# Second mixer of a two-layer backbone: recurrent unit moved under the tiles of the input product, attention with two units' scores in PSUM and the heads' norm in two batches

## The chip, the cores and the metric

The kernel is one program on one core of a Trainium2 chip, written against the engines themselves: each engine (TensorE or PE, VectorE or DVE, ScalarE or ACT, GpSimd or POOL, and SyncE or SP, which issues DMAs) runs its own list of instructions in order, and the lists meet only at semaphores (`wait_ge`, `then_inc`). The metric is the device time of one execution in microseconds (us), as the median of some runs. There are no other cores to wait for.

## What is computed

Two layers over 512 latent and 256 context tokens of width 1024, in fp32. The part that matters here is the mixer of the second layer, between that layer's two half feed-forward blocks:

```python
gate, xr, q, k, v = split(hx @ w_in, (512,) * 5)            # and the same of the context's hc
xr = dwconv_centred(xr, conv_w, conv_b)                     # 4 taps
h  = rglru_bidir(xr, ...)   # r = sigmoid(x wa + ba), i = sigmoid(x wx + bx), a = exp(-8 r softplus(-lam)),
                            # b = sqrt(1 - a^2) * i * x, h_t = a_t h_(t-1) + b_t, both directions, context first
out_c = gelu(gate) * h
q, k = rms_norm(q), rms_norm(k)                             # per head of 64; then rotary embedding
s = q k^T / 8;  p = softmax(s)                              # 4 heads x 2 halves, 512 queries x 768 keys
w = p[:, 0] - lam * p[:, 1];  o = w v
o = rms_norm(o, subln_g) * (1 - lam_init)
y = concat(out_c, o) @ w_out
```

## The kernel before

Activations lie transposed in SBUF: 8 chunks of 128 channels by 768 tokens (`x`, and `xh`, `xl` for the normed input). Every product is done as three fp32r passes: a value is split into a high part (rounded to fp32r) and the rest, and PE adds high x high, low x high and high x low. So each weight tile of 128 columns comes by DMA into `raw`, ACT copies it to `wh` (`split_hi`, line 961, after the product of the tile two places earlier), DVE subtracts to get `wl` (`split_lo`, line 1424), and PE runs the tile (`gemm`): 8 steps k of three passes, into one of two PSUM buffers `G[0]`, `G[1]` (two banks each). Tiles alternate between the two slots, so tile t+2 can start only when ACT and DVE have split its weights and somebody has emptied `G` (`psum_free`). A tile over all 768 tokens is laid out in `HALVES`; one over the 512 latent tokens alone is `LSEG`.

The second mixer is three functions on each engine. `cd_in_*` is the input product, 20 tiles: v, k, q, the recurrent input xr, the gate. Tiles 0 and 1 start on the unnormed input, 2 and 3 are staggered with the norm (`gemm_unnormed`, `gemm_staggered`). Beside the tiles run the turning of v to tokens, the head norms of k and q (`Square` L1281, head sums on PE L815 to L819 into `NP`, `Ln` L1250 and `Exp` L1253 in `rs`, the product in `kq_norm` L1875), the rotary embedding (`swap` L830, `rotate`), the convolution (`conv`, L1898 and L1900) and, at the end, gelu. `cd_mid_*` is everything between the two products. Its order is written out by hand in `SCHED`: for each of four channel groups p of the recurrent unit four attention units with the unit's steps laid between them. A step of the recurrent unit for both directions d: `gates` (PE L849, fp32, sigmoid on ACT L1317), `decay` (exp and tanh, L1325 and L1327), a square on POOL L2159, `comp` (DVE L1948), `root` (sqrt L1332), a product on POOL L2163, `scan` (DVE L1956 to L1968), then `gated`, `hi`, `lo`. The sigmoids of group p+1 wait for the scan of group p (`lru_h`), since they write the same buffers. An attention unit a (a block of 128 queries and a head): both halves' scores on PE (L862, fp32, 64 rows deep, one half in rows 0 to 63 and one in 64 to 127 of the array) into `G[0]` and `G[1]`; DVE's maxima (L1988, one each); two Exp on ACT from PSUM (L1344); on DVE reciprocal, factor and the weighted difference `wb` (L1997, L1999, L2004); six turns on PE (L870); ACT copies them to SBUF (L1350); six products with v (L879); DVE scales the result (L1983); ACT squares and sums it (L1357). Scores of unit a wait for the Exp of unit a-1, because there is one place for them. DVE takes the maxima of a before the difference of a-1. After the last unit all 16 sums of squares go through one Ln and Exp (L1372, L1373), DVE norms four blocks (L2023), PE turns them (L898), DVE and ACT write the second half of the output product's input (L2029, L1376, L2033). `cd_out_*` is the output product, 8 `LSEG` tiles, the first two interleaved; its steps k < 4 need the recurrent half, k >= 4 the attention half.

Each ACT function set must be loaded when it changes (`ACT_TABLE_LOAD`): sigmoid, exp with tanh, sqrt, gelu and Ln have rows of their own.

## Time and profile before

| | us |
|---|---|
| median of 3 runs (2982.64 to 2988.03) | 2984.38 |
| the profiled execution, device time | 2982.56 |
| its span, first to last instruction | 2980.8 |
| PE busy, of the span | 95% |
| DVE, ACT, POOL busy | 52%, 36%, 19% |
| input product of the second mixer, from the end of tile 3 | 2287.0 to 2414.7 |
| between the products | 2414.7 to 2567.4 |
| mean granted TensorE clock | 0.981 |

The profile's page says where the time goes by engine, and which slices of the span have PE below nine tenths; the windows say the same of one stretch. A row of the timeline is: start, duration, engine, line, operation, output and inputs, count, and in brackets the idle time before it and what ended it. A row of the groups is: line, engine, operation, shapes, count, busy time, mean ns of one, idle time before it. Merged rows ("x2", "x6") run from the first start to the last end. An fp32 matmul has two records.

### The profile page before, as it was taken

To read this page: it belongs to the slowest core of one execution; us is meant where nothing else is said; L and a number is where in the kernel's file an instruction comes from. 1 tells how busy PE (TensorE), PEld (TensorE's weight loads), DVE (VectorE), ACT (ScalarE), POOL (GpSimd) and SP (SyncE) were. 2 spreads that over 40 slices of the span, in tenths; PEclk is the share of its full clock that TensorE was granted. 3 is DMA by queue.
4 is the path that set the end of the run, shared out by engine and by line. 5 is a ranking of instruction groups with operands and counts; after the bars stand their busy time and mean duration, and the time that the engine had idled before them with its cause. 6 is when DMAs were issued, how large, how long until landed. Compare 5 with 4: busy or idle time off the path is not lost.

```text
span 2980.8 us, 40958 instructions
## 1 busy us (share of the span) xinstructions
PE 2818.3 (95%) x15780; PEld 2631.5 (88%) x15780; DVE 1549.7 (52%) x2035; ACT 1083.2 (36%) x1514; POOL 570.0 (19%) x294
## 2 busy tenths in 40 slices
PE   5999999999977789999999999999999987799999
PEld 5899999998965778999999999999999855688887
DVE  6964366454556856662565542222246557753333
ACT  3432144236455334441343322112224657442221
POOL 2441044200012721440342100000020113200000
PEclk8999999999999899999999999999999989999999
DMA  7343144111210012441343112111211110123232
GB/s 298 129 159 120 59 152 163 65 50 51 71 42 1 1 36 95 165 166 67 122 153 108 55 64 66 68 56 63 69 58 64 57 57 1 39 92 102 92 97 101
DMA packets 67672, 258.77 MB, mean 87 GB/s; under 512 B 7424, under 2 KB 8576, under 8 KB 66944
## 3 DMA queue, kind: packets, MB, share of 16 engines
q1 hardware_dynamic: 50016, 192.58, 19.4%
q10 hardware_dynamic: 17568, 65.02, 6.3%
q8 instruction: 55, 0.90, 0.1%
q14 instruction: 33, 0.27, 0.0%
HBM read 255.47 MB, written 2.10 MB: 86 GB/s over the span
## 4 chain that ended last, share of the span: by engine, by line
PE 83%; DVE 9%; ACT 2%; issue 2%; POOL 1%; DMA 0%; DVEq 0%; ACTq 0%; POOLq 0%
PE G L450 20%; PE G L452 20%; PE G L454 20%; PE G L457 5%; PE G L459 5%; PE G L461 5%; DVE B L1429 1%; DVE tmp L1613 1%; DVE sL L1829 1%; DVE wl L1424 1%; PE NP L757 1%; PE G L849 1%; DVE xl L1605 1%; PE NP L666 1%; DVE sL L1820 0%
## 5 line engine op out<-in xcount | busy, mean ns | idle before, releaser
L961 ACT ACTIVATE wh<-raw 128x1024 fp32r<-128x1024 f32 (+1 forms) x300 | 338.9, 1130 | 1540.5 <-PE G L454 1227.4
L450 PE MATMUL G<-xh,wh 128*128 128x384 f32 x2624 | 673.8, 337 | 34.3 <-DVE wl L1424 21.9
L452 PE MATMUL G<-xl,wh 128*128 128x384 f32 x2624 | 670.2, 336 | 0.0
L454 PE MATMUL G<-xh,wl 128*128 128x384 f32 x2624 | 669.2, 336 | 0.0
L1424 DVE TENSOR_TENSOR wl<-raw,wh 128x1024 fp32r<-128x1024 f32 (+1 forms) x300 | 427.0, 1423 | 379.5 <-ACT wh L961 378.7
L450 PEld LDWEIGHTS G<-xh,wh 128*128 128x128 f32 x2624 | 474.8, 189 | 40.8 <-DVE wl L1424 19.0
L452 PEld LDWEIGHTS G<-xl,wh 128*128 128x128 f32 x2624 | 477.3, 189 | 0.0
L454 PEld LDWEIGHTS G<-xh,wl 128*128 128x128 f32 x2624 | 476.9, 189 | 0.0
L2094 POOL TENSOR_TENSOR mraw<-mraw,scb 128x1024 f32<-128x1024 f32 x120 | 315.0, 2625 | 646.7 <-DVE B L1429 646.7
L454 PE MATMUL G<-hh,wl 128*128 128x384 f32 x1056 | 268.1, 334 | 0.0
L452 PE MATMUL G<-hl,wh 128*128 128x384 f32 x1056 | 268.1, 334 | 0.0
L450 PE MATMUL G<-hh,wh 128*128 128x384 f32 x1056 | 268.0, 334 | 0.0
L1429 DVE SCALAR_TENSOR_TENSOR B<-mraw,scb 128x1024 f32<-128x1024 f32 x120 | 235.2, 1960 | 0.0
L1531 DVE SCALAR_TENSOR_TENSOR x<-G,modG,x 128x256 f32<-128x256 f32 x112 | 49.0, 479 | 349.3 <-PE G L454 349.3
L1459 DVE TENSOR_TENSOR tmp<-tmp,G 128x768 f32<-128x768 f32 x64 | 61.1, 954 | 284.8 <-PE G L454 284.8
L457 PE MATMUL G<-xh,wh 128*128 128x512 f32 (+1 forms) x528 | 199.7, 388 | 2.8 <-DVE wl L1424 2.8
L461 PE MATMUL G<-xh,wl 128*128 128x512 f32 (+1 forms) x528 | 197.6, 384 | 0.0
L459 PE MATMUL G<-xl,wh 128*128 128x512 f32 (+1 forms) x528 | 197.6, 384 | 0.0
L452 PEld LDWEIGHTS G<-hl,wh 128*128 128x128 f32 x1056 | 190.7, 188 | 0.0
L450 PEld LDWEIGHTS G<-hh,wh 128*128 128x128 f32 x1056 | 190.7, 188 | 0.0
L454 PEld LDWEIGHTS G<-hh,wl 128*128 128x128 f32 x1056 | 190.6, 188 | 0.0
L977 ACT ACTIVATE mraw<-mraw 128x1024 f32<-128x1024 f32 x120 | 126.3, 1053 | 42.3 <-ACT mraw L977 23.6
(332 smaller groups left out, 3256.8 us busy)
## 6 DMA issues: line engine op xcount, KB each, us to landing
raw<-in_w SPq DMA_DIRECT2D x176, 512.0 KB, 3.5
mraw<-in_wmn ACTq DMA_DIRECT2D x120, 512.0 KB, 4.5
raw<-in_w SPq DMA_DIRECT2D x64, 704.0 KB, 4.0
raw<-in_abin SPq DMA_DIRECT2D x24, 512.0 KB, 3.5
raw<-in_cdin SPq DMA_DIRECT2D x20, 512.0 KB, 3.5
mini<-in_wmn SPq DMA_DIRECT2D x9, 512.0 KB, 14.8
gmini<-in_wmn SPq DMA_DIRECT2D x2, 2048.0 KB, 21.9
raw<-in_about SPq DMA_DIRECT2D x8, 512.0 KB, 3.5
```

Of the source, the lines that this page charges most:

```text
L450: pe.matmul(bank(h), W, tokens(rh, h), start=(k == 0), stop=False)
L452: pe.matmul(bank(h), W, tokens(rl, h), start=False, stop=False)
L454: mm = pe.matmul(bank(h), L, tokens(rh, h), start=False, stop=(k == nk - 1))
L457: pe.matmul(G[slot][:, a:b], W, rh[:, k, a:b], start=(k == 0), stop=False)
L459: pe.matmul(G[slot][:, a:b], W, rl[:, k, a:b], start=False, stop=False)
L461: mm = pe.matmul(G[slot][:, a:b], L, rh[:, k, a:b], start=False, stop=(k == nk - 1))
L961: act.activation(wh[slot][:, 0:nk * P], raw[slot][:, 0:nk * P], ACT.Copy).then_inc(hi_done, 1)
L977: act.activation(mraw[:, j, :], mraw[:, j, :], ACT.Copy, accum_out=M[:, bass.ds(it * 3 + (24 + j), 1), 1:2].rearrange("p a s -> p (a s)")) ...
L1424: dve.tensor_tensor(wl[slot][:, 0:nk * P], raw[slot][:, 0:nk * P], wh[slot][:, 0:nk * P].bitcast(F32), ALU.subtract).then_inc(lo_done, 1)
L1429: return dve.scalar_tensor_tensor(B67[:], tile, 1.0, scv[:, s, :], ALU.mult, ALU.mult, accum_out=out)
L1459: dve.tensor_tensor(by_block(hf[:, 0:T]), by_block(g1s[:, 0:T]), from_banks(G[1], 0, T), ALU.mult).then_inc(psum_free[1], 1)
L2094: pool.tensor_tensor(mraw[:, j, :], mraw[:, j, :], scb[:, 1, :], ALU.mult).then_inc(mod_prod, 1)
```

## The change

All of it is in the second mixer.

- The tiles of the input product come in the order xr, gate, k, q, v (0 to 3, 4 to 7, 8 to 11, 12 to 15, 16 to 19). Convolution and recurrent unit run beside tiles 2 to 13: each engine's steps stand in a list by tile c; PE's gate matmuls, head sums, swaps and two of four turns of v stand between steps k of a tile, at places given by four tables. The gate matmuls go into `NP` and `B67`. `SCHED` is gone.
- DVE now waits in `cd_in` for the scan of a group before it empties the next tile's PSUM, since the list is in order. POOL does its eight rotary products after all its products of the recurrent unit.
- The weights of the gates come as six DMAs into the unused ends of `raw`, `wh`, `wl`, ahead of tile 4's weights.
- The constants' arithmetic and its two small Exp move into the feed-forward block before.
- In the attention the eight banks are cut anew: three banks of scores for even units, three for odd ones (`SC`), and `B67` for turns and values. Scores are six matmuls of 256 keys, alternating between the two halves and never in the same bank, in two parts around `values(a - 3)`. One maximum instruction takes both halves. DVE's order is: difference of a-1, scaling of a-3, maxima of a. A turn waits for the scaling of the unit before (`on_done`), a copy on ACT goes ahead of the Exp.
- The norm of the heads is done for units 0 to 11 at once while the last units run and for the last four after them; the last block is turned between steps 3 and 4 of the output product. ACT and DVE write the output product's input straight from PSUM. The recurrent half of it lies in `gateh` and `hsuml`.

```diff
+        lruw = [at(f"lruw{q}", [P, FH * P - D], MR + 3 * D + q * FH * P + D) for q in range(6)]
...
+        banks = ctx.enter_context(nc.psum_tensor("banks", [P, 4096], F32))
+        G = [banks[:, 1024 * s:1024 * s + 1024] for s in range(2)]
+        NP, B67 = banks[:, 2048:3072], banks[:, 3072:4096]
+        SC = [banks[:, 1536 * q:1536 * q + 1536] for q in range(2)]
...
-        SCHED = []
...
+        GATES_IN = {4: 0, 7: 1, 9: 2, 11: 3}
+        SUM_AT = {(10, 3): 0, (12, 2): 1, (13, 4): 2, (14, 4): 3, (15, 2): 4, (16, 2): 5, (17, 2): 6, (18, 2): 7}
+        SWAP_AT = {(13, 5): 0, (14, 5): 1, (15, 6): 2, (16, 4): 3, (17, 1): 4, (18, 0): 5, (19, 0): 6, (19, 6): 7}
+        TURN_AT = {(19, 2): 0, (19, 5): 1}
...
+            load_tiles(CD + 2, 2, dr["cdin"], KC, 2)
+            for q in range(6):
+                wq = FH * P - D
+                n = min(wq, 16 * P - q * wq)
+                sp.dma_start(lruw[q][:, 0:n], dr["lruw"][:, q * wq:q * wq + n]).then_inc(lruw_landed, 16)
+            load_tiles(CD + 4, CD_IN_T - 4, dr["cdin"], KC, 4)
...
+            def gates(p_, d):
+                e = 2 * p_ + d
+                if e == 0:
+                    pe.wait_ge(lruw_landed, 96)
+                pe.wait_ge(cv_ready, 8 + p_ + 1)
+                if e == 6:
+                    pe.wait_ge(kq_ln, 8 + 1)
+                for g in range(2):
+                    if e:
+                        pe.wait_ge(gate_sig, 2 * (e - 1) + g + 1)
+                    m = 8 * g + 4 * d + p_
+                    for a, b, _s in SEGS:
+                        mm = pe.matmul((NP, B67)[g][:, a:b], lruw[m // 3][:, m % 3 * P:m % 3 * P + P], xc[:, p_, a:b],
+                                       start=True, stop=True)
+                    mm.then_inc(gate_mm, 1)
...
+            def head_sum(i):
...
+                if i < 4:
+                    pe.wait_ge(sql_set, 8 + i + 1)
+                    for a, e, _s in SEGS:
+                        pe.matmul(NP[:, a:e], blkr[:], sqh[:, a:e], start=True, stop=False)
+                        mm = pe.matmul(NP[:, a:e], blkr[:], sql[:, a:e], start=False, stop=True)
...
+                for c in range(4, CD_IN_T):
+                    def under(k):
+                        if c in GATES_IN and k in (2, 6):
+                            gates(GATES_IN[c], k // 4)
+                        if (c, k) in SUM_AT:
+                            head_sum(SUM_AT[c, k])
+                        if (c, k) in SWAP_AT:
+                            swap(SWAP_AT[c, k])
+                        if (c, k) in TURN_AT:
+                            turn_v(TURN_AT[c, k])
+                    gemm(CD + c, c % 2, (CD + c) // 2, KC, xh, xl, LSEG if 4 <= c < 8 or 12 <= c < 16 else HALVES, under)
...
+                def scores(a, part):
...
+                        if (s, b_) == (1, 0):
+                            pe.wait_ge(s2_bank, a + 1)
+                        mm = pe.matmul(SC[a % 2][:, T * s + b_:T * s + b_ + 256], q2[hp, h, P * qt:P * qt + P],
+                                       k2[hp, h, b_:b_ + 256], start=True, stop=True)
+                        if (s, b_) == (0, 512):
+                            mm.then_inc(s2_bank, 1)
+                    if part:
                         mm.then_inc(s2_done, 1)
...
                 def turn(a):
                     pe.wait_ge(w_done, a + 1)
                     if a:
-                        pe.wait_ge(wt_ready, a)
+                        pe.wait_ge(on_done, a)
+                    else:
+                        pe.wait_ge(v2_ready, 4)
...
+                for a in range(NA2 + 3):
+                    if a < NA2:
+                        scores(a, 0)
+                    if 3 <= a:
+                        values(a - 3)
+                    if a < NA2:
+                        scores(a, 1)
+                    if a == 0:
+                        turn_v(2)
+                        turn_v(3)
+                    if 2 <= a <= NA2 + 1:
+                        turn(a - 2)
+                    if a == NA2 + 1:
+                        turn_o(0)
+            def turn_o(qt):
+                pe.wait_ge(onr_done, qt + 1)
+                if qt >= 2:
+                    pe.wait_ge(cd_cat2, qt - 1)
+                for h in range(4):
+                    mm = pe.transpose(NP[:, 512 * (qt % 2) + P * h:512 * (qt % 2) + P * h + P], onq[qt][:, P * h:P * h + P],
+                                      cst("ident"))
+                mm.then_inc(oq_done, 1)
...
+                    if f == 2 and h == 0:
+                        act.wait_ge(dl_set, 1)
+                        act.activation(coef[:, 1, :], coef[:, 0, :], ACT.Exp, scale=-1.0).then_inc(coef_exp, 1)
+                        act.wait_ge(dl_set, 3)
+                        act.activation(dl[:, 2:4], dl[:, 0:2], ACT.Exp).then_inc(dl_exp, 1)
...
+                act.wait_ge(xn_ready, 40)
+                act.wait_ge(coef_set, 1)
+                for c in range(2, CD_IN_T):
+                    split_hi(CD + c + 2, c % 2, (CD + c + 2) // 2, KC)
+                    if c < 4:
+                        evac(c)
+                    if 4 <= c < 8:
+                        gelu(c - 4)
+                    if c == 2:
+                        add_bias(0)
+                    if c == 3:
+                        gates(0)
+                    if c == 4:
+                        root(0)
+                        add_bias(1)
+                        add_bias(2)
+                    if c == 5:
+                        add_bias(3)
+                    if c == 6:
+                        gates(1)
+                        hi(0)
+                    if c == 7:
+                        root(1)
+                    if c == 8:
+                        squares(0)
+                        squares_hi(0)
+                        gates(2)
+                        hi(1)
+                    if c == 9:
+                        root(2)
+                        squares(1)
+                        rs(0)
+                        squares_hi(1)
+                    if c == 10:
+                        gates(3)
+                        squares(2)
+                        hi(2)
+                    if c == 11:
+                        root(3)
+                        rs(1)
+                        squares_hi(2)
+                    if c == 12:
+                        rs(2)
+                        squares(3)
+                        squares_hi(3)
+                        hi(3)
+                    if 13 <= c < 18:
+                        rs(c - 10)
+                    if 13 <= c < 17:
+                        squares(c - 9)
+                    if c == 18:
+                        copy_v(0)
+                        copy_v(1)
...
                 def att(a):
...
                     if 2 <= a <= NA2 + 1:
                         act.wait_ge(tr2_done, a - 1)
                         if a >= 4:
                             act.wait_ge(pv2_done, a - 3)
-                        act.activation(wtb[a % 2][:], NP[:, 0:T], ACT.Copy).then_inc(wt_ready, 1)
+                        act.activation(wtb[a % 2][:], B67[:, 0:T], ACT.Copy).then_inc(wt_ready, 1)
+                    if a < NA2:
+                        act.wait_ge(max2_ready, a + 1)
+                        if a >= 2:
+                            act.wait_ge(w_done, a - 1)
+                        for s in range(2):
+                            act.activation(pr2[a % 2][s][:], SC[a % 2][:, T * s:T * s + T], ACT.Exp, bias=st2[:, a % 4, s:s + 1],
+                                           accum_out=st2[:, a % 4, 2 + s:3 + s]).then_inc(p2_ready, 1)
                     if a >= 4:
...
+                        head_squares(a - 4)
...
+                copy_v(2)
+                for a in range(NA2):
+                    att(a)
+                    if a == 0:
+                        copy_v(3)
+                head_norm(0, 12)
+                att(NA2)
+                att(NA2 + 1)
+                hi(0)
+                head_squares(NA2 - 2)
+                hi(1)
+                head_squares(NA2 - 1)
+                head_norm(12, 16)
+                hi(2)
+                hi(3)
...
+                dve.wait_ge(xn_ready, 40)
+                for q in range(2):
+                    for a, b in ((0, 2), (514, 517), (773, 774)):
+                        dve.memset(xpad[q][:, a:b], 0.0)
+                for q in range(2, 4):
+                    ins = dve.memset(xpad[q][:], 0.0)
+                ins.then_inc(pad_zero, 1)
+                conv(0)
+                for c in range(2, CD_IN_T):
+                    if c >= 8:
+                        evac(c)
+                    split_lo(CD + c + 2, c % 2, KC)
+                    if c in (2, 3):
+                        conv(c - 1)
+                    if c == 4:
+                        comp(0)
+                        conv(3)
+                    if c == 5:
+                        scan(0)
+                    if c == 6:
+                        gated(0)
+                    if c == 7:
+                        comp(1)
+                        lo(0)
+                        scan(1)
+                    if c == 8:
+                        squares_lo(0)
+                        gated(1)
+                    if c == 9:
+                        comp(2)
+                        lo(1)
+                        scan(2)
+                    if c == 10:
+                        squares_lo(1)
+                        kq_norm(0)
+                        gated(2)
+                    if c == 11:
+                        comp(3)
+                        lo(2)
+                        scan(3)
+                    if c == 12:
+                        squares_lo(2)
+                        kq_norm(1)
+                        gated(3)
+                    if c == 13:
+                        squares_lo(3)
+                        lo(3)
+                    if 13 <= c < 19:
+                        kq_norm(c - 11)
+                        rotate(c - 13)
+                    if c >= 18:
+                        rotate(c - 12)
...
+                for a in range(NA2 + 2):
+                    if 1 <= a <= NA2:
+                        weigh(a - 1)
+                    if a >= 3:
+                        out(a - 3)
+                    if a < NA2:
+                        biggest(a)
+                    if a == NA2:
+                        normed(0)
+                normed(1)
+                normed(2)
+                out(NA2 - 1)
+                out_lo(0)
+                out_lo(1)
+                normed(3)
+                out_lo(2)
+                out_lo(3)
...
-    order = [(4 * gw, 5 * gw), (3 * gw, 4 * gw), (2 * gw, 3 * gw), (gw, 2 * gw), (0, gw)]
+    order = [(gw, 2 * gw), (0, gw), (3 * gw, 4 * gw), (2 * gw, 3 * gw), (4 * gw, 5 * gw)]
```

## Rows read from the trace of the kernel before

**Rows 1.** Windows: busy us (instructions) of each engine, granted clock, DMA share, GB/s.

```profile
2287.00:2414.60 127.60, 126.32 (x641) 111.81 (x639) 70.29 (x91) 71.22 (x86) 11.97 (x8) 1.00 0.24 78
2414.60:2568.00 153.40, 110.99 (x499) 71.78 (x499) 106.57 (x142) 109.28 (x181) 43.29 (x24) 0.87 0.01 4
```

**Rows 2.** Timeline, PE, at the two edges of the stretch between the products.

```profile
2416.41 2.82 PE L849 MATMUL G<-xc,lruw 128*128 128x512 f32 x8 [1.74 <-issue]
...
2579.38 0.39 PE L461 MATMUL G<-xh,wl 128*128 128x512 f32 x1
```

**Rows 3.** Timeline of attention units between the products: DVE, ACT and PE.

```profile
2504.13 1.80 DVE L1988 TENSOR_REDUCE st<-G 128x1 f32<-128x768 f32 x2
...
2505.10 0.90 ACT L1344 ACTIVATE pb<-G,st 128x768 f32<-128x768 f32 x1 [1.01 <-DVE st L1988]
...
2506.29 1.02 DVE L2004 SCALAR_TENSOR_TENSOR wb<-pb,st,pb 128x768 f32<-128x768 f32 x1
2506.78 0.20 ACT L1344 ACTIVATION_READ_ACCUMULATOR pb<-G,st 128x1 f32 x1
...
2506.87 0.81 ACT L1350 ACTIVATE wtb<-NP 128x768 f32<-128x768 f32 x1
...
2507.83 0.34 DVE L1983 TENSOR_SCALAR onq<-B,st 128x128 f32<-128x128 f32 x1
...
2530.46 1.57 PE L862 MATMUL G<-k,q 64*128 64x512 f32 x8
...
2531.96 0.87 PE L870 MATMUL NP<-con,wb 128*128 128x128 f32 x6
...
2532.67 1.50 PE L879 MATMUL B<-vtok,wtb 128*128 128x128 f32 x12
```

**Rows 4.** Timeline, DVE, at the end of the attention: the wait for the heads' norm.

```profile
2562.46 2.50 DVE L2023 TENSOR_TENSOR onq<-onq,hrs 128x512 f32<-128x512 f32 x4 [3.69 <-ACT hrs L1373]
```

**Rows 5.** Timeline of the recurrent unit's steps between the products.

```profile
2419.31 0.90 ACT L1317 ACTIVATE lR<-G,par 128x768 f32<-128x768 f32 x1
2420.26 2.85 PE L849 MATMUL G<-xc,lruw 128*128 128x512 f32 x8 [1.04 <-ACT lR L1317]
...
2430.32 0.93 ACT L1327 ACTIVATE lR<-lR,coef 128x768 f32<-128x768 f32 x1
...
2502.13 1.81 DVE L1948 SCALAR_TENSOR_TENSOR lR<-lX,lR 128x768 f32<-128x768 f32 x2
...
2507.98 1.28 ACT L1332 ACT_TABLE_LOAD   x1
2509.27 1.58 ACT L1332 ACTIVATE lR<-lR 128x768 f32<-128x768 f32 x2
2510.20 4.28 POOL L2163 TENSOR_TENSOR lI<-lI,lR 128x768 f32<-128x768 f32 x2 [8.80 <-ACT lR L1332]
2510.26 2.55 DVE L2004 SCALAR_TENSOR_TENSOR wb<-pb,st,pb 128x768 f32<-128x768 f32 x1
...
2519.05 1.28 ACT L1317 ACT_TABLE_LOAD   x1 [4.03 <-DVE hsum L1968]
```

**Rows 6.** Timeline beside the input product: splits, convolution and head norm.

```profile
2397.15 3.14 DVE L1900 SCALAR_TENSOR_TENSOR cb<-pad,par,cb 128x771 f32<-128x771 f32 x3
...
2398.42 1.06 ACT L961 ACTIVATE wh<-raw 128x1024 fp32r<-128x1024 f32 x1 [2.66 <-PE G L461]
...
2400.21 1.22 DVE L1424 TENSOR_TENSOR wl<-raw,wh 128x1024 fp32r<-128x1024 f32 x1
...
2403.86 1.06 ACT L961 ACTIVATE wh<-raw 128x1024 fp32r<-128x1024 f32 x1 [0.50 <-PE G L461]
```

**Rows 7.** Timeline, PE, after a wait for split weights.

```profile
2272.76 0.80 PE L450 MATMUL G<-xh,wh 128*128 128x384 f32 x2 [1.60 <-DVE wl L1424]
...
2276.51 0.51 PE L450 MATMUL G<-xh,wh 128*128 128x384 f32 x2
2276.86 0.51 PE L452 MATMUL G<-xl,wh 128*128 128x384 f32 x2
```

More of the change, by code:

```diff
@@ L206, in build @@
         wtb = [at(f"wtb{q}", [P, T], ATT[q] + 3 * T) for q in range(2)]
-        ovb = [at(f"ovb{s}", [P, 512], TB + s * T) for s in range(2)]
         fw = [FREE]
@@ new lines, in turn_o, with step @@
+            def turn_o(qt):
[6 more added lines that the diff above has]
+                mm.then_inc(oq_done, 1)
+            def cd_out_pe():
+                def step(s, k):
+                    return gemm_step(s, k, KC, gateh if k < 4 else xh, hsuml if k < 4 else xl, LSEG)
+                for s in range(2):
+                    weights_ready(CDO + s, s, CDO // 2)
+                turn_o(1)
+                turn_o(2)
+                for k in range(KC):
@@ L1360, in cd_mid_act @@
-                for what, i in SCHED:
-                    if what == "gates":
-                        gates(i)
-                    if what == "decay":
-                        decay(i)
-                    if what == "root":
-                        root(i)
-                    if what == "hi":
-                        hi(i)
-                    if what == "att":
-                        att(i)
-                act.wait_ge(ss_ready, NA2)
-                chain(act.activation(hsq[:, 1, :], hsq[:, 0, :], ACT.Ln, bias=eps[:, 0:1], scale=1.0 / P))
```

478 lines of the change are left out of this document (195 added, 283 removed).

## Prediction

> **What bounds it now.** I read the windows first, then the timeline at their edges, then single units of work. Beside the input product PE is the bound: from the end of tile 3 it is busy 126 of 127.6 us, ACT 71, DVE 70 [rows 1]. Between the products nothing is full: in 153 us PE is busy 111 at a mean clock of 0.87, ACT 109, DVE 107 [rows 1]; there the lists wait for one another. The stretch begins at 2414.7 (1.74 us before its first matmul) and with the first two output tiles, which both kernels interleave, ends at 2579.8 [rows 2]: 165.1 us. So work taken out of it and laid beside the tiles pays twice where PE has room, and costs PE time one for one where it hasn't.
>
> **Part 1, the attention alone.** I follow one unit through the new order. DVE takes the maxima of unit a in one instruction; two of 768 last 1.80 us, one of 1536 I take as 1.70 (bounds 1.6 and 1.8). From the first Exp's start to the end of the second's sum ACT needs 1.88 us; from the end of maxima over reciprocal and factor to the end of the difference DVE needs 1.38; the scaling 0.34, of which 0.26 stands ahead of the next instruction [rows 3]. In DVE's new list the difference of a stands before the maxima of a+1, and waits for both Exp of a. So a second place for scores frees PE, but not the chain maxima, Exp, Exp, difference, scaling, maxima: 1.70 + 1.88 + 1.38 + 0.26 and two hand-overs between DVE and ACT of 0.06 each are 5.35 us a unit (5.1 to 5.7). Everything else fits in: PE needs 1.6 + 0.75 + 1.5 = 3.9 [rows 3]; turn (0.9) and copy (0.7) run while DVE takes the maxima, and end about when these do, so they add 0 to 0.3. The Trainium skill (TensorEngine Tiling (Array Packing), Restrictions and Gotchas) says that different row tiles cannot access the same PSUM bank at the same time; the new six-part order keeps to that, and eight score records in 1.57 us show the halves side by side; had they to go one after the other, 2.6 us, PE would still fit.
>
> First maxima: PE is free of tile 19, DVE empties it (1.1), splits a tile (1.2) and does the last rotation (1.4): 3.8 us after tile 19. Then 15 periods, two of them without scaling: 3.8 + 2 x 5.1 + 13 x 5.35 = 83.6. From the last unit's maxima on: Exp 3.6; the square of the unit before and the first batch's norm, 3.7 as now [rows 4], to 7.4; copy 8.0, values and scaling of 14 to 10.1, turn, copy, values and scaling of 15 to 13.9; two turns of blocks and eight steps of the output product (0.68 each) to 20.7, under which the second batch's norm (to 18.4) hides; the last block's turn, copy and difference hold PE 1.6; the rest ends at 28. So 112 us against 165.1: **-53.3** (-48 to -56).
>
> **Part 2, what PE gets beside the tiles.** Eight times two gate products at 2.8 us [rows 5]: +22.4. Two of four turns of v go the other way (-1.6). Head sums, swaps, tiles are the same number. **+20.8.** The constants go beside the feed-forward block, where DVE and ACT have idle time; the two Exp bring two table loads: nothing on the path (1 us at most, if a weight split came behind them). The six DMAs stand on SP's queue ahead of tile 4's weights, which are wanted some 10 us later: nothing.
>
> **Part 3, who waits beside the tiles.** ACT's list from tile 4 to step 4 of tile 13 holds 9 splits (1.0), 16 sigmoids (0.8 to 0.9), 16 exp and tanh (0.93), 8 square roots (0.8), about 18 loads (1.28) [rows 5, 6] and some 16 us of gelu, bias, squares and norms: 82 us. PE's own work there is 87 us, tiles, gates and two head sums. So nearly each us that ACT waits for somebody is one that PE waits. I walk the lists with those durations, in us from the start of tile 4. A tile is 5.44 (`LSEG`, the time from one split's start to the next's, [rows 6]) or 24 pairs of passes at 0.35 [rows 7], split high 1.06 and low 1.22, conv 3.8 [rows 6]. POOL and DVE hold each other: the difference L2004, 1.02 alone, takes 2.55 beside POOL's product [rows 5, 3], it ends 0.8 after the first of two 1.8 us products; a scan queued at the same time waits for the second.
> - Group 0: gates end at 9, ACT's chain of exp and tanh at 15. Only then come the high part of tile 6 and gelu, at 18. PE has finished tile 5 at 16: **2.0**. Square root, then two biases; the last conv waits for the first of these, the low part of tile 7 for the conv: 28.3, PE waits **4.8**.
> - Group 1: scan of group 0 ends 33, sigmoids behind it, exp and tanh done 45, root 51, POOL 55, scan 59. Tile 8 is finished at 49, and DVE's copy of it stands behind the scan, ACT's square behind the copy, the sigmoids of group 2 behind the square: the gates at step 6 of tile 9 wait 57.8 to 64.2: **6.4**.
> - Groups 2 and 3: the gates of group 3 wait for a Ln that reads `NP`: **1.0**. Scan of group 2 ends 87; of group 3, 112. Tile 12 is finished at 101; PE waits **1.4** for tile 13's low part, then at step 4 for the head sum 2, whose operand DVE makes behind that scan, a copy and a split, at 115: **10.2**. Head sum 3 waits **1.5** in tile 14. From tile 15 on ACT keeps up.
> These are 27.3. Behind a wait of 1.60 us PE runs at its lower level, 1.2 GHz: a pair of passes takes 0.80, and 0.51 again (2.4 GHz) only 3.75 us later [rows 7], which has cost about 1.7 us. Behind the other wait shown, 1.74 us [rows 2], it ran at the upper one. I charge 1.7 to each of the three waits over 4 us: 5.1. Sum **+32.4**; bounds: 16, if every second wait is covered by something that I put too late, and 46.
>
> A rule of the Trainium skill speaks against this part: ScalarE: Activation LUTs, What ACT_TABLE_LOAD costs, gives 1283 ns and a drain of about 1380 ns more for each switch. Here the instruction behind a load starts 1.29 us after it [rows 5]: the trace has the first part and not the second. Were the drain paid in the walk's list, its 13 loads more than now would add 18 us.
>
> **Sum.** 2982.56 (the profiled execution, 1.8 under the median of the runs) - 53.3 + 20.8 + 32.4 = 2982.5. I take **2982**: what the attention gives, the input product takes.
>
> **Rivals.**
> - *The recurrent round is shorter than I walk it* (0.32). For it: PE is the bound of the input product now, its lists have slack, and 27 us of waits rest on four places where one list stands behind another, each of which goes if gelu, conv, the copy of tile 8 or the operand of head sum 2 comes 4 to 10 us earlier. Against: sigmoids of p+1 can't start before the scan of p, 16.8 us after the gates even without other work (0.9 + 1.28 + 3.7 + 2.1 + 0.8 + 3.6 + 4.5) [rows 5]. Waits of 16: 2966; none at all: 2950.
> - *VectorE and GpSimd hold each other on the path* (0.28, slower). POOL has 24 instructions of 1.5 to 1.8 us in the walk, DVE's splits, comp and head norm read two operands from SBUF. Today most meet beside waits. If eight more of DVE's path instructions queue behind one of POOL's at 1.5 us, +12, and one more restart at the lower clock, +1.7: 2996. It decides from about four such meetings (+6).
> - *The change doesn't do what it says in the attention*: the two places for scores don't shorten the chain. That is in my sum. Were they to (4.6 a unit, PE and DVE alone), -12: 2970. I give it 0.05, within the first.
>
> **How the numbers follow.** Walk as computed 0.40, within 6 us mostly (faster 0.10, same 0.24, slower 0.06); first rival 0.32 (0.28, 0.04, 0); second 0.28 (0, 0.06, 0.22). Faster 0.38, same 0.34, slower 0.28, where 0.2% (6 us) is what a measurement of this kernel tells from no change. Signs are mixed: the likeliest case alone has 2974 to 2990. The range for 8 in 10 reaches to the other cases: 2957 to 3004.
>
> **What would show it.** Between the products: Exp to Exp 5.35 us apart, PE not the one waited for, clock near 1; 112 us from tile 19 to the end of the second output tile. Beside the input product: 181 us instead of 127.7 from tile 4 on; PE waits for `wl` before tile 7, for a sigmoid in tile 9, for `sql` in tile 13, the last the longest; ACT busy nearly throughout up to tile 13. I am wrong if PE has no wait over 3 us there (then 2960 or less), or if the units come more than 6 us apart (then over 2993).

## The result and the profile after

The changed kernel takes 2990.22 us (median of 20 runs, 2985.55 to 2993.08), the kernel before 2984.56 in the same comparison (20 runs, 2981.75 to 2988.03): ratio 1.0017, 95% interval 1.0010 to 1.0023. It is 5.7 us slower. I had said 2982 and called a gain a little likelier than a loss, so the sign was wrong and the size off by 8; the range of 2957 to 3004 holds it. A second comparison gave 2989.68 against 2983.61, 1.0021 (1.0012 to 1.0030). The profiled execution of the changed kernel is one of its short ones, 2985.62 us (span 2983.8); to that of before (2982.56) it is +3.06, where my sum had -0.1. Two single executions of variants below, 8424.85 us (head sum 2's operand) and 4028.16 us (passes for nothing), lie in a slower state and bear on nothing; without them the medians of these two fall by 0.1 and 0.2.

Windows of the changed kernel (from, to, span; busy us and instructions of TensorE; granted clock; DMA share; GB/s): from the start of tile 4 to the end of the input product, then to the end of the second output tile. They answer to [rows 1] and [rows 2].

```profile
2287.00:2467.00 180.00, 152.53 (x691) 0.94 0.16 50
2467.00:2583.00 116.00, 89.55 (x559) 0.96 0.02 5
```

180 us instead of 127.7, and 116 instead of 165.1: more exactly they are 180.8 (2286.57 to 2467.37) and 115.5 (to 2582.86), and I had walked 181 and 112. What TensorE waited for between 2284 and 2620 (line that waits <- what it waits for: us in total, times, longest; `onq` is a unit's scaled result, `sql` the low part of the squares for a head sum, `wl` the low part of a tile's weights, `lR` a sigmoid's output):

```profile
PE banks L889 <- DVE onq L2161: 15.7, 14, 3.2
PE banks L811 <- DVE sql L2035: 12.0, 2, 10.7
PE banks L453 <- DVE wl L1516: 8.5, 4, 4.8
PE banks L798 <- ACT lR L1340: 6.1, 1, 6.1
```

The waits beside the input product one by one (timeline, TensorE: start, us, operation, [idle before <- releaser]):

```profile
2305.11 0.47 PE L453 MATMUL banks<-xh,wh 128*128 128x512 f32 x1 [2.15 <-ACT gate L1317]
2315.65 0.79 PE L453 MATMUL banks<-xh,wh 128*128 128x512 f32 x1 [4.84 <-DVE wl L1516]
...
2351.19 5.23 PE L798 MATMUL banks<-xc,lruw 128*128 128x512 f32 x8 [6.06 <-ACT lR L1340]
2370.77 2.82 PE L798 MATMUL banks<-xc,lruw 128*128 128x512 f32 x8 [1.13 <-issue]
2390.13 0.50 PE L453 MATMUL banks<-xh,wh 128*128 128x512 f32 x1 [1.21 <-DVE wl L1516]
2403.93 0.77 PE L811 MATMUL banks<-sqh,blkr 128*128 128x512 f32 x1 [10.74 <-DVE sql L2035]
2413.99 0.47 PE L811 MATMUL banks<-sqh,blkr 128*128 128x512 f32 x1 [1.26 <-DVE sql L2035]
```

In this order they are tile 6, tile 7, gates in tile 9, gates of group 3, tile 13, head sum 2 and head sum 3: walked 2.0, 4.8, 6.4, 1.0, 1.4, 10.2, 1.5. The second number of a row is how long the pass behind the wait takes. For one pass of 512 columns 0.79 and 0.77 are the lower clock level, 0.39 to 0.50 the upper; for the eight records of the gates 5.23 and 2.82.

A unit of the attention (timeline, VectorE, ScalarE and TensorE; it answers to [rows 3]):

```profile
2504.75 1.75 DVE L2167 TENSOR_REDUCE st<-banks 128x2 f32<-128x1536 f32 x1
2504.98 0.85 PE L889 MATMUL banks<-con,wb 128*128 128x128 f32 x6 [0.88 <-DVE onq L2161]
2505.86 0.81 ACT L1424 ACTIVATE wtb<-banks 128x768 f32<-128x768 f32 x1 [2.51 <-PE banks L889]
2506.57 0.90 ACT L1430 ACTIVATE pb<-banks,st 128x768 f32<-128x768 f32 x1
2507.45 0.90 ACT L1430 ACTIVATE pb<-banks,st 128x768 f32<-128x768 f32 x1
2508.47 0.17 DVE L2148 RECIPROCAL st<-st 128x2 f32<-128x2 f32 x1 [1.98 <-ACT pb L1430]
2508.93 1.02 DVE L2155 SCALAR_TENSOR_TENSOR wb<-pb,st,pb 128x768 f32<-128x768 f32 x1
2509.86 0.35 DVE L2161 TENSOR_SCALAR onq<-banks,st 128x128 f32<-128x128 f32 x1
2510.12 1.75 DVE L2167 TENSOR_REDUCE st<-banks 128x2 f32<-128x1536 f32 x1
```

Maxima, Exp, Exp, reciprocal, difference, scaling, maxima: 2504.75 to 2510.12, 5.37 us (walked 5.35), and the copy behind the turn ends about when the Exp starts (2506.67 and 2506.57).

### The profile page after: what moved, and what is told of

Same layout as the page of the kernel before. It is cut to its first block, busy times and chain, and to the rows that moved or that the text cites. A ratio compares the mean times of both kernels' runs of the same rounds, so it can differ in the third digit from the quotient of the medians.

```text
span 2983.8 us, 41082 instructions
## 1 busy us (share of the span) xinstructions
PE 2810.1 (94%) x15844; PEld 2631.5 (88%) x15844; DVE 1540.4 (52%) x2023; ACT 1111.1 (37%) x1531; POOL 571.5 (19%) x294
## 4 chain that ended last, share of the span: by engine, by line
PE 81%; DVE 9%; issue 3%; ACT 3%; POOL 1%; DMA 0%; DVEq 0%; ACTq 0%; POOLq 0%
PE banks L446 20%; PE banks L450 20%; PE banks L448 20%; PE banks L453 5%; PE banks L457 5%; PE banks L455 5%; DVE banks L1521 1%; DVE wl L1516 1%; DVE tmp L1705 1%; DVE sL L1925 1%; DVE xl L1697 1%; PE banks L798 1%; ACT pb L1430 1%; PE banks L753 1%; PE banks L662 1%
## 5 line engine op out<-in xcount | busy, mean ns | idle before, releaser
L446 PE MATMUL banks<-xh,wh 128*128 128x384 f32 x2624 | 675.9, 338 | 32.0 <-DVE wl L1516 20.1
L448 PE MATMUL banks<-xl,wh 128*128 128x384 f32 x2624 | 669.8, 336 | 0.0
L450 PE MATMUL banks<-xh,wl 128*128 128x384 f32 x2624 | 669.3, 336 | 0.0
L446 PEld LDWEIGHTS banks<-xh,wh 128*128 128x128 f32 x2624 | 474.8, 189 | 41.5 <-DVE wl L1516 17.7
L448 PEld LDWEIGHTS banks<-xl,wh 128*128 128x128 f32 x2624 | 477.2, 189 | 0.0
L450 PEld LDWEIGHTS banks<-xh,wl 128*128 128x128 f32 x2624 | 477.1, 189 | 0.0
L448 PE MATMUL banks<-hl,wh 128*128 128x384 f32 x1056 | 267.9, 334 | 0.0
L446 PE MATMUL banks<-hh,wh 128*128 128x384 f32 x1056 | 267.9, 334 | 0.0
L450 PE MATMUL banks<-hh,wl 128*128 128x384 f32 x1056 | 267.8, 334 | 0.0
L1521 DVE SCALAR_TENSOR_TENSOR banks<-mraw,scb 128x1024 f32<-128x1024 f32 x120 | 237.4, 1978 | 0.0
```

The costliest lines, as they stand in the source:

```text
L446: pe.matmul(bank(h), W, tokens(rh, h), start=(k == 0), stop=False)
L448: pe.matmul(bank(h), W, tokens(rl, h), start=False, stop=False)
L450: mm = pe.matmul(bank(h), L, tokens(rh, h), start=False, stop=(k == nk - 1))
L1521: return dve.scalar_tensor_tensor(B67[:], tile, 1.0, scv[:, s, :], ALU.mult, ALU.mult, accum_out=out)
```

## The experiments

Four reorderings of the changed kernel, run together. Since executions differ by 1 to 3 us before tile 4 already, I compare two stretches of the profiles as well: from the start of tile 4 to the first scores (2286.57 to 2468.46 in the changed kernel, 181.9), and from there to the step k = 4 of the output product (to 2577.12, 108.7). By the medians the first three reorderings are 5.0, 6.7 and 5.9 us under the changed kernel's 2990.22, where the expectations had 6 to 9, 3 to 5 and about 4; that median is of another comparison (the kernel before had 2984.56 there and 2983.83 here), and the medians hold the changing clock of other places too, so I go by the first stretch.

**Head sum 2's operand ahead of the scan.**

```diff
 ScalarE, c == 11:  -root(3) rs(1) squares_hi(2)   +rs(1) squares_hi(2) root(3)
 ScalarE:           -hi(3) at c == 12              +hi(3) at c == 13
 VectorE, c == 11:  -comp(3) lo(2) scan(3)         +comp(3) lo(2) squares_lo(2) kq_norm(1)
 VectorE, c == 12:  -squares_lo(2) kq_norm(1) gated(3)   +scan(3) squares_lo(3) gated(3)
```

> The operand of head sum 2 is made in front of the scan of group 3 (ScalarE: Ln, Exp and high part of the squares in front of the last square roots; VectorE: the low part in front of scan(3), the gated product of group 3 and its high part later). My walk: in the changed kernel TensorE stands 10.7 us in tile 13 for sql; here sqh is ready near 2393.9 and sql near 2394.9 on the clock of that profile, TensorE's wait becomes about 1.8, head sum 3 waits about 2 instead of 1.3, and the kernel is about 8 us faster than the changed one (6 to 9), at about 2982. If the wait is not from the order of the lists but from VectorE and GpSimd holding each other, scan(3) and the product before it only move and sql is late again: the wait stays over 6 us and the time within 3 us of the changed kernel.

2985.21 us (before 2983.83), the first stretch 178.6: 3.3 less, where I had expected 8 (6 to 9).

```profile
2395.63 0.47 PE L811 MATMUL banks<-sqh,blkr 128*128 128x512 f32 x1 [1.91 <-DVE sql L2036]
2408.75 0.77 PE L811 MATMUL banks<-sqh,blkr 128*128 128x512 f32 x1 [5.82 <-DVE sql L2036]
```

The wait for head sum 2 went from 10.7 to 1.9 as walked, so this wait came of the order. But head sum 3 now waits 5.8 (I had said 2): its operand stands behind the moved scan, and GpSimd's products run beside three of that scan's four passes, which take 2.33, 2.14 and 1.69 instead of 0.68, 1.28 and 0.67. Half of the 8.8 us was a debt to the next sum.

**Tile 8's copy in front of scan(1).**

```diff
+                    if c == 8:
+                        scan(1)
                     split_lo(CD + c + 2, c % 2, KC)
...
                     if c == 7:
...
-                        scan(1)
```

> VectorE copies tile 8 out of PSUM in front of scan(1) instead of behind it. My walk: ScalarE's squares and their high part no longer stand between the end of the scan (2346.2) and the sigmoids of group 2, which start there instead of at 2350.1; TensorE's wait in tile 9 falls from 6.1 to about 2.2 us, everything behind it keeps its distances, so about 4 us faster than the changed kernel (3 to 5), 2986. If the walk is wrong and the wait rests on the gates' own chain (exp, tanh, root, product, scan) alone, the wait stays at 5 to 6 and the time moves by under 1.5 us.

2983.48 us; first stretch 178.6, 3.3 less; TensorE's wait in tile 9 is 3.54 instead of 6.06 (I had expected 2.2), and the gate products behind it run at the upper clock (2.82 instead of 5.23):

```profile
2352.34 2.82 PE L798 MATMUL banks<-xc,lruw 128*128 128x512 f32 x8 [3.54 <-ACT lR L1340]
```

**The last convolution behind the low part of tile 8.**

```diff
 VectorE:  -conv(3) behind comp(0), c == 4      +conv(3) in front of gated(0), c == 6
 ScalarE:  -add_bias(3) at c == 5               +add_bias(3) behind gates(1), c == 6
```

> The last convolution goes behind the low part of tile 8 and the scan of group 0 in VectorE's list, its bias on ScalarE behind the gates of group 1. My walk: the low part of tile 7 is ready at 2312.1 instead of 2315.6, TensorE's wait there 4.8 -> 1.3 us, scan(0) and with it all later groups come 3.6 us earlier: 3.6 us, and 1 more if the restart at the lower clock (0.63 instead of 0.39 a pass) goes with it: 2985 to 2987. If the chain of the groups were not what sets the later waits, the gain would be eaten in tile 9, whose wait would grow from 6.1 to over 9 us: no change in the time.

2984.36 us; first stretch 178.5, 3.4 less. Tile 7 waits 2.09 now (expected 1.3), for gelu, and tile 9 waits the same 6.08 as before the edit: the gain was not taken back, so the chain of the groups sets the later waits and moved with the scan.

```profile
2315.15 0.47 PE L453 MATMUL banks<-xh,wh 128*128 128x512 f32 x1 [2.09 <-ACT gate L1317]
2350.34 4.89 PE L798 MATMUL banks<-xc,lruw 128*128 128x512 f32 x8 [6.08 <-ACT lR L1340]
```

**Maxima in front of the weights.**

```diff
+                    if a >= 3:
+                        out(a - 3)
+                    if a < NA2:
+                        biggest(a)
                     if 1 <= a <= NA2:
                         weigh(a - 1)
-                    if a >= 3:
-                        out(a - 3)
-                    if a < NA2:
-                        biggest(a)
```

> In the attention VectorE takes the maxima of unit a in front of the weights of unit a-1 (scaling of a-3, maxima of a, reciprocal, factor and difference of a-1). My theory: the unit's period of 5.37 us is the chain maxima, Exp, Exp, difference, scaling, maxima; with the new order the maxima of a run beside the Exp of a-1, no chain closes within one unit, and TensorE is the bound (scores 1.6, turn 0.75 to 0.9, values 1.6): period 4.0 to 4.3 us, 15 times 1.2 = 18 us less, at 2971 to 2974. Rival: not the chain but something shared (PSUM banks, the copy between turn and values, values behind scaling) sets it: period over 4.9, 7 us or less.

2970.06 us against 2983.83 before (0.9955, 0.9942 to 0.9967), 20 less than the changed kernel. Through the middle units TensorE works without a gap, and a unit takes 4.46 us (2500.32 to 2504.78), a little over the 4.0 to 4.3 I expected because the scores take 2 x 1.06 and not 1.6:

```profile
2500.32 1.13 PE L875 MATMUL banks<-k,q 64*128 64x256 f32 x6
2501.38 0.88 PE L889 MATMUL banks<-con,wb 128*128 128x128 f32 x6
2502.18 1.13 PE L875 MATMUL banks<-k,q 64*128 64x256 f32 x6
2503.24 1.60 PE L896 MATMUL banks<-vtok,wtb 128*128 128x128 f32 x12
2504.78 1.13 PE L875 MATMUL banks<-k,q 64*128 64x256 f32 x6
```

So the 5.37 us was the chain, closed by VectorE's order alone. The second stretch is 90.3, 18.4 less, and that this is my 15 x 1.2 is partly luck: from the first maxima to the last, twelve periods give 0.91 each, the first three units 5.2, and 2.1 is a fall of the clock in the changed kernel (below) that doesn't come here.

**The changed kernel once more.**

> The changed kernel, unaltered, beside the others of this call. Its twenty times lay in two groups, seven from 2985.6 to 2987.2 and thirteen from 2988.4 to 2993.1, and its profile is of the lower one (2985.6). If the groups belong to the kernel, its median is again 2989 to 2991 and a profile of the upper group shows 3 to 5 us more at one place: by my theory of the clock at TensorE's restarts (passes at 0.63 instead of 0.39 us behind a wait) that is one or two waits more that are followed by the lower clock, between 2284 and 2600. If they belong to the chip or the hour, the median is near 2986.

2989.68 us (ten runs, 2987.4 to 2992.3), and this profile is of a long execution, 2990.95: 5.3 us over the other. No single place has them: tile 4 starts 1.4 later, the first stretch is 1.2 longer, the second 1.1, the rest 1.6. The last is seen best. Both profiles wait 1.9 us for the weights of the second pair of output tiles; in the first one all passes behind take 0.39 to 0.50, in this one:

```profile
2588.47 0.50 PE L453 MATMUL banks<-gateh,wh 128*128 128x512 f32 x1 [1.90 <-DVE wl L1516]
...
2589.35 0.63 PE L453 MATMUL banks<-gateh,wh 128*128 128x512 f32 x1
...
2592.68 0.40 PE L457 MATMUL banks<-gateh,wl 128*128 128x512 f32 x1
```

3.3 us at the lower level, which costs 1.6. The same wait is followed by the lower level in one execution and not in the other. The twenty executions of the changed kernel say the same as a whole: the mean granted clock is 0.982 to 0.985 in the seven that take under 2988 us, and 0.978 to 0.983 in the thirteen above. So the two groups belong to the kernel, as I expected.

**Passes for nothing in two waits.**

```diff
+            def fill(n):
+                for _ in range(n):
+                    pe.matmul(NP[:, 0:512], blkr[:], xh[:, 0, 0:512], start=True, stop=True)
...
+                if i == 2:
+                    fill(37)
...
+                    if c == 7:
+                        pe.wait_ge(gate_sig, 4)
+                        fill(19)
```

> The changed kernel with passes whose result nobody reads laid into two of TensorE's waits: 19 in front of tile 7 (wait 4.8 us) and 37 in front of head sum 2 (10.7 us), at 0.23 us each, so that they end before what TensorE waits for is there. The waits' ends stay where they are. By the theory of the restart the passes behind them then last 0.39 us from the first on instead of 0.63 to 0.79, which is worth 1.2 to 1.7 us at each place: 2.5 to 3.5 us less in the profile, and if the upper group of the times is made by restarts, the spread goes and the median is 2984 to 2986. If the clock is not what makes the difference, the time stays within 1 us of the changed kernel's median of the same call.

2986.45 us, 3.2 less than the changed kernel beside it. The passes behind both waits run at the upper level from the first on (0.79 and 0.77 before):

```profile
2311.17 4.60 PE L804 MATMUL banks<-xh,blkr 128*128 128x512 f32 x19
2316.17 0.50 PE L453 MATMUL banks<-xh,wh 128*128 128x512 f32 x1 [0.40 <-DVE wl L1525]
...
2394.18 8.90 PE L804 MATMUL banks<-xh,blkr 128*128 128x512 f32 x37 [1.80 <-ACT ssq L1303]
2403.11 0.50 PE L817 MATMUL banks<-sqh,blkr 128*128 128x512 f32 x1
...
2412.53 0.47 PE L817 MATMUL banks<-sqh,blkr 128*128 128x512 f32 x1 [2.09 <-DVE sql L2044]
...
2413.45 0.63 PE L453 MATMUL banks<-xh,wh 128*128 128x512 f32 x1
```

By the end of tile 14's passes in front of head sum 3 TensorE is 3.0 us ahead of the changed kernel, as expected of the clock (2.5 to 3.5). But there it waits 2.09 instead of 1.26, and behind this wait the clock falls, which it did not in the changed kernel's profile, and takes 1.6 back. So the first stretch is 181.4, only 0.5 less than in the short profile of the changed kernel and 1.7 less than in the long one. The passes for nothing keep the clock up where they stand, and the next wait can take the gain again; that the medians are 3.2 apart is more than these profiles show. The spread stayed (2983.4 to 2989.3), since the other waits are left, and the median lies above the 2984 to 2986 that I had expected.

**The product in front of the scans on VectorE.**

```diff
 GpSimd:   -lI[d] = lI[d] * lR[d]   for d in 0, 1
 VectorE:  +lI[d] = lI[d] * lR[d]   for d in 0, 1, at the head of scan(p_)
```

> The product in front of the scans (beta times gated input, two of 768 columns per group) goes from GpSimd (1.8 us each) to VectorE. It tests the rival of VectorE and GpSimd holding each other: in the changed kernel the first scan lasts 2.3 us instead of 0.68 in groups 1, 2 and 3, queued behind GpSimd's second product. On VectorE the two products take 1.0 each, the second right behind the first, and the four scans follow: the end of the group's scans comes 1.5 to 2 us earlier in groups 0 to 3. Since the groups' chain sets the waits of tile 9 and head sum 2, TensorE's waits shrink by the same and the sum is 4 to 7 us less than the changed kernel. If the chain did not set them, nothing changes (within 1 us).

2979.72 us (0.9988 of before, 0.9979 to 0.9997), 10 less than the changed kernel beside it (expected 4 to 7); first stretch 175.5, 6.4 less. Of the changed kernel, then of this one (GpSimd and VectorE, group 1):

```profile
2338.11 3.61 POOL L2323 TENSOR_TENSOR lI<-lI,lR 128x768 f32<-128x768 f32 x2 [5.04 <-ACT lR L1352]
2339.97 2.30 DVE L2064 TENSOR_TENSOR_SCAN lX<-lA,lI 128x256 f32<-128x256 f32 x1 [2.40 <-POOL lI L2323]
```

```profile
2337.26 1.83 DVE L2062 TENSOR_TENSOR lI<-lI,lR 128x768 f32<-128x768 f32 x2 [0.51 <-ACT lR L1352]
2339.00 0.68 DVE L2068 TENSOR_TENSOR_SCAN lX<-lA,lI 128x256 f32<-128x256 f32 x1
```

The scan of 256 columns takes 0.68, and 2.30 while GpSimd's second product runs: it ends at 2342.27, 0.55 us behind GpSimd's products (2341.72). TensorE's waits in tile 7, tile 9 and at head sum 2 fell by 1.7, 1.7 and 2.5.

**The unit left out.**

```diff
-        GATES_IN = {4: 0, 7: 1, 9: 2, 11: 3}
+        GATES_IN = {}
...
-    conv, add_bias, gates, root (ScalarE), comp, scan, GpSimd's products
+    gated: hsum = gate * gate
```

> The changed kernel without the recurrent unit: the gate products, sigmoids, exp, tanh, roots, convolutions, scans and GpSimd's three products per group are left out (the square of the gelu stands in for the unit's output, its split and the six weight transfers stay). Tiles, head sums, swaps and the whole attention are as in the changed kernel. It prices the second side of my sum by itself. By the walk the unit costs 22.4 us of TensorE and 32.4 of waits and restarts beside the tiles: 54.8 less, 2935, with 127 from the start of tile 4 to the first scores instead of 181.9, and no wait of TensorE over 1.6 us there. By the changed kernel's trace (gate pair 2.39 apart, waits 28.0) 19.1 + 28.0 + 2 to 5: 49 to 52 less, 2938 to 2941. If the input product had waits of its own under the unit's (splits, head norms with their table loads), 40 or less: over 2950.

2932.08 us, 58 less by the medians and 53.7 by the profiles; tile 4 to first scores is 129.5, 52.4 less. I had walked 54.8, the trace had given 49 to 52. Two waits for `sql` are left, 2.8 together, the longer 2.1, where I had said none over 1.6 (us in total, times, longest):

```profile
PE banks L809 <- DVE sql L2031: 2.8, 2, 2.1
```

**All together.** The diffs are those above: first the four reorderings, then these and the product on VectorE.

> The four reorderings together (operand of head sum 2 in front of scan(3); copy of tile 8 in front of scan(1); last convolution behind tile 8's low part; maxima in front of the weights). Each alone took, between the start of tile 4 and the first scores, 3.1, 3.3 and 3.4 us, and the last one 18.4 between the first scores and the output product. If they rest on different waits they add: 28 us less than the changed kernel, about 2961. If they share waits (what the convolution gives is taken again in tile 9 or at head sum 2), 22 to 24 us: 2966.

2960.38 us. The stretches are 172.2 and 90.3: 9.7 and 18.4 less, where each alone gave 3.3, 3.3, 3.4 and 18.4. They rest on different waits.

> The four reorderings of the run with all of them, and the product in front of the scans on VectorE. If the shortened chain of a group still sets the waits that are left (2.1 in tile 7, 3.5 in tile 9, 4.2 at head sum 3), it gives most of what it gave alone, 6.4 us between the start of tile 4 and the first scores: 2954. If the reorderings have used the same slack, 2 to 3: 2958.

2956.18 us, **0.9908 of before (0.9894 to 0.9922)**, first stretch 167.5: 4.7 less than the last one, between the two expectations.

The other tail, on top of that:

```diff
 ScalarE:  -head_norm(0, 12) att(16) att(17) hi(0) head_squares(14) hi(1) head_squares(15) head_norm(12, 16) hi(2) hi(3)
           +att(16) att(17) head_squares(14) head_squares(15) head_norm(0, 16) hi(0) hi(1) hi(2) hi(3)
 TensorE:  -turn_o(0) turn_o(1) turn_o(2), k = 0 to 3, turn_o(3), k = 4 to 7
           +k = 0 to 3, turn_o(0) turn_o(1) turn_o(2) turn_o(3), k = 4 to 7
 VectorE:  -normed(0) before the last two out(), out_lo(0) out_lo(1) before normed(3)
           +out(15), normed(0) to normed(3), out_lo(0) to out_lo(3)
```

> As the run before it, with another end of the attention: one head norm for all sixteen heads instead of two batches, behind the copy of the last unit, and the four first steps of the output product in front of the turns of the heads' output. In the changed kernel ScalarE's Ln, Exp and their two table loads stand between the last Exp and the copy of unit 14, and TensorE waits 3.2 us there, with its passes at the lower clock behind it (values of unit 14 2.5 to 2.9 us instead of 1.6). By my theory of the tail the copy of 14 comes 3.5 us earlier, the last values end near 4.5 us earlier, the four steps (5.5 us) cover the norm, and the step for k = 4 starts 3.5 to 4.5 us earlier: 4 us less. Rival: the norm of the last unit and the chain of four turns, copies and differences is longer than the four steps, and what was saved ahead is waited for behind: 1 us or less, or slower.

2956.27 us, no gain (expected 4 less). The second part did get shorter, 87.8 against 90.3, but behind the new waits for the turned blocks (1.2 and 1.6) stands

```profile
2544.55 0.50 PE L453 MATMUL banks<-xh,wh 128*128 128x512 f32 x1 [1.56 <-DVE xl L2178]
...
2545.62 0.63 PE L453 MATMUL banks<-xh,wh 128*128 128x512 f32 x1
```

and seven passes in all take 0.63, which gives 1.5 of the 2.5 back. The first stretch is 1.4 longer than in the run before, by another such fall: the gates of tile 9 take 4.51 behind a wait of 2.02, and in the run before 2.82 behind the same wait. So the rival had the number, 1 us or less, but its mechanism only in part: the new waits cost some of what I had hoped for, and the clock, in this profile, the rest.

## Why the prediction was right, and where it was wrong

- *What bounds the kernel, and part 3's walk*: right. The seven waits beside the tiles sum to 27.4 (walked 27.3), each in its place and behind the work I had named; tile 4 got one more of 0.56. Three reorderings moved three of them, the run without the unit all but 2.8. The charge of 5.1 for restarts held as well: against the same passes at the upper level, those behind the waits lose 1.3 in tile 7, 2.4 in tile 9 and 1.5 at head sum 2, 5.2 together. From tile 4 to the end of the product it is 180.8, walked 180.9; that this fits to 0.1 is partly luck, see part 2.
- *Part 2*: the eight records of two gate products last 2.8, but they overlap with what stands behind: the second tile pass starts 2.81 after the first of them (2323.79 to 2326.60), where the tile's own step is 0.23. So a pair costs 2.6 and eight of them 21, and 22.4 was 1.6 too high. Some 1.8 us that I had in no term, such as first passes behind waits of 0.47 to 0.50 instead of 0.39, made it up; I have not placed all of them.
- *Part 1, the unit*: right. 5.37 for 5.35, with the chain as named, and the counter-test of the maxima's place (4.46).
- *Part 1, the rest*: **this is the step that failed.** I wrote that TensorE needs 3.9 of the 5.35 us and "everything else fits in", and charged restarts at the lower clock to three waits beside the tiles and to none in the attention. TensorE's own need is 4.46, which at the upper clock still fits: in ten units it waits 0.88 and the period stays 5.37. But behind the wait of 3.23 between the fourth maxima and the fifth its clock fell to the lower level (granted clock 0.83 between 2480 and 2500, 1.00 between 2500 and 2520), and that unit took 7.5:

```profile
2486.53 1.75 DVE L2167 TENSOR_REDUCE st<-banks 128x2 f32<-128x1536 f32 x1
2486.76 1.51 PE L889 MATMUL banks<-con,wb 128*128 128x128 f32 x6 [3.23 <-DVE onq L2161]
2488.20 2.07 PE L875 MATMUL banks<-k,q 64*128 64x256 f32 x6
2490.20 2.73 PE L896 MATMUL banks<-vtok,wtb 128*128 128x128 f32 x12
2494.03 1.76 DVE L2167 TENSOR_REDUCE st<-banks 128x2 f32<-128x1536 f32 x1 [0.70 <-PE banks L875]
...
2560.99 2.93 PE L896 MATMUL banks<-vtok,wtb 128*128 128x128 f32 x12 [1.42 <-ACT wtb L1424]
```

  Turn, the first half of the scores and values take 6.3 instead of 3.6, and the next maxima stand behind them: 2494.03 instead of 2491.90, +2.1. The values of unit 14 behind a wait of 1.42 take 2.93 instead of 1.60, +1.3. These 3.4 are the 115.5 us between product and second output tile against my 112, and with that all of the 3.1 by which the profile is over my sum. In the run with the maxima in front of the weights, the waits in the middle are gone and no unit there runs at the lower level; only the values of unit 14 do, behind a wait of 3.20. In the long profile of the changed kernel the fall comes behind waits of 0.90 as well:

```profile
2564.22 2.93 PE L896 MATMUL banks<-vtok,wtb 128*128 128x128 f32 x12 [0.90 <-ACT wtb L1424]
```

  No run laid passes for nothing into these waits, so what the fall costs here is read from the rows and not from an experiment.
- *The sum against the median*: I had put the profiled execution 1.8 under the median. In the changed kernel it is 4.6 under, in the one before 2.0. My sum starts from the profiled execution, and I gave its result as the median: 1.8 us of the 8.2 are this slip, since a sum of -0.1 means 2984.3 for the median, no change. The other 2.6 to 2.8 I take for restarts that this execution happened to be spared: the long profile has more of them from tile 4 on in all three parts, 3.9 us together, and the granted clock of the twenty executions goes the same way. I charged the lower clock to three waits over 4 us; it follows waits of 0.9 to 3.2 as well, in some executions.
- *The drain of about 1380 ns that the Trainium skill adds to a table load* (ScalarE: Activation LUTs, What ACT_TABLE_LOAD costs): the trace disagrees, in the changed kernel too, where the Ln of the heads' norm starts at 2558.41 behind a load from 2557.11 to 2558.39. I left it out, and the walk's waits sum to 27.3 where the trace has 27.4.
- *Rivals*: a shorter round (0.32) didn't come: beside the tiles TensorE has three waits over 3 us. VectorE and GpSimd do hold each other on the path, and taking one meeting per group away gave 6.4 in the profile, but the walk had it priced, it was no addition. The slower side was right for a reason that I had not among the rivals: a clock that falls in the waits which a hidden chain leaves. My 0.28 for slower stood on another mechanism.
- *What would show it*: unit, first stretch, the places of the waits and their order hold. ScalarE is busy 86.2 of the 117.4 us up to head sum 2, not "nearly throughout". "Clock near 1" between the products did not hold (0.96 in the short profile, 0.91 in the long one), and that line should have been a rival with a price.

What stays open: which waits are followed by the lower level. 1.90 in one place was and wasn't, and so were 2.02 in tile 9 of two runs. The Trainium skill (TensorE: Matmul & The Clock Gate, Part 1) says that the gate's phase does not start with the kernel and that the number of slow passes therefore differs between runs; the two profiles agree in that it differs, and no run here shows the cause.

## What to carry over

Price TensorE's restarts wherever a list leaves it waiting once a unit, not only behind the longest waits, and check with a second profile: two executions of one program differed by 5.3 us, 3.9 of them from tile 4 on, where the rows show the clock behind it. Bring a sum that starts from a profiled execution back to the median before you call it a forecast. In a software pipeline look for the one engine whose order closes the loop within a unit; here a second place for scores left the period at the chain's 5.37 us until VectorE took the maxima of the next unit before the weights of this one, which was worth 18 us, 2 of them by a fall of the clock that it avoided. Walking the lists with durations of the trace found the waits to 0.5 us, so use it before the change to place the steps, not only to forecast it.

## What the runs showed of the hardware

- A wait of TensorE can be followed by passes at the lower clock level and need not be: behind 1.90 us in one place and 2.02 in another it was so in one execution and not in another. A fall costs 1.3 to 2.4 us here, and in the changed kernel such falls set the two profiled executions 3.9 us apart from tile 4 on.
- Passes that nobody reads, laid into a wait of 10.7 and one of 4.8 us, keep the upper clock level: the first pass behind takes 0.50 instead of 0.77 to 0.79, and TensorE is 3.0 us ahead when it comes to the next wait. There the clock fell instead, for 1.6. The medians are 3.2 apart.
- A scan of 256 columns on VectorE takes 0.68 alone and 2.3 while GpSimd runs a product of 768 columns from SBUF; it went away when the product moved to VectorE. The Trainium skill (SBUF — State Buffer, SBUF: two separate sides) has a VectorE instruction with two inputs in SBUF and a GpSimd instruction that reads SBUF exclude each other on a shared pair of ports, each for the whole instruction, and these rows agree.
- The scores' passes of 64-row halves for one unit hold TensorE 1.50 us up to the next instruction in one go (2468.46 to 2469.96 in the changed kernel) and 2 x 1.06 when they are issued in two parts (2500.32 to 2501.38, 2502.18 to 2503.24).
